# Two chunks instead of one left for the block-by-block end of a section's opening

## The chip, the cores and the metric

The kernel runs on one core of a Trainium2 chip, in one launch. The metric is the device time of a run in microseconds; the median of the timed runs is given. Lower is better.

## What is computed

The reference passes an activation `x` of 512 tokens by 1024 channels, in float32, through a chain of residual layers. Cut to what matters here:

```
layer 0:  x += 0.5 * norm(swiglu(norm(x)))      ffn0     w_gate, w_up: 1024 x 2816, w_down: 2816 x 1024
          x += norm(attention(norm(x)))         attn     w_in: 1024 x 3072 (stick-breaking and dilated heads)
          x += 0.5 * norm(swiglu(norm(x)))      ffn1
layer 1:  ffn2, mLSTM mixer (w_in: 1024 x 4112, a causal convolution of 4 taps, chunked memory), ffn3
layer 2:  x += mixer(norm(x))                   even     pooling and a diagonal state-space scan
layer 3:  x += mixer(norm(x))                   odd      gate, depthwise convolution of 31 taps, layer norm
end:      norm(x)
```

Almost all of the arithmetic is matrix products of `x` (or a hidden activation) with a weight of 1024 rows or more.

## The kernel before

**Products.** Activations are kept transposed: `x` is eight chunks of 128 channels (partitions) by 512 tokens. A weight is cut into blocks, each giving 128 output channels from all 1024 input channels: eight 128 x 128 tiles, 512 KB. To be exact enough, both factors are split into a high part (rounded to fp32r) and a low part (the rest), and each tile's product is three matmuls, high*high, low weight*high activation, high weight*low activation (`product3`, L1929 to L1931). So a block is 8 x 3 = 24 matmuls into one PSUM bank; its last one raises `blocks_done`.

**The weights' pipeline.** Blocks pass through a ring of four slots. SP (the SyncE queue) loads block b into slot b mod 4 once block b-4 is done (`load`, L1945); ACT makes the high part `wh` (`high_part`, L378); POOL makes the low part `wl` (`low_part`, L386), which raises `w_split`; the tensor engine waits for that before it takes the block. Each engine takes its work strictly in the order in which it is written, so the SILU or the copy that ACT has ahead of a `high_part` also holds that one up.

**The activations' split.** At the start of a section the eight chunks of the normalized input are made one after another: ACT makes the high part `xh` (L2199 and L2200 in the FFNs and attention, where the norm's rate is applied to the products later; L408 in the others) and POOL the low part `xl` (`split_low`, L417), which raises `xn_ready`. Between chunk 4 and chunk 5 POOL makes the low part of the section's block 3.

**A section's opening.** As the chunks arrive one by one, the first three blocks of a section (slots 0, 1 and 2) are not taken block after block but chunk by chunk, in the function `first_three`: for chunk k the six matmuls with the high activation (`three_high`, L1996 and L1997: three blocks, two matmuls each), one step behind it the three with the low activation (`three_low`, L2002). The last chunk is taken block by block (`three_last`, through `product3`): three matmuls and block 0 is done, three more and block 1, three more and block 2. `first_three` opens ten sections: the gate and up projections of ffn0 to ffn3, attn.qk, mlstm.qk, even.in, even.out, odd.in, odd.out. The output section of the memory layer (`memory_out`) and that of attention (`attention_out`) have openings of their own, which call the same helpers.

**Behind the opening** comes, in the FFNs and in attention, `spread_rate` (L1882), which brings the norm's rate into a PSUM bank; DVE copies it (L2388) and needs the copy to scale the first product. Then come block 3 and, when its slot 0 has been loaded and split again, block 4, and so on in order. In an FFN, ACT's order after the opening is: SILU of the first hidden tile (L2214), `high_part` of block 4, the hidden tile's high part (L2218), `high_part` of block 5. In mlstm.qk DVE does a convolution of four taps on each block and ACT a SILU of it before the next `high_part`. In even.out and odd.out ACT squares the new `x` chunk of block 0 before it takes block 4.

Of the kernel before, what the change touches and what calls it, by code (L numbers as in the profile page):

```python
# [15 lines left out]
KD = D // P  # L16
# [100 lines left out]
def build(nc, x_in, weights, vecs, consts, rel_bias, buckets, w_gates, pool_w, bst, cst, scratch, turn, park, out):  # L117
    ctx = ExitStack()
    with ctx:
# [1806 lines left out]
        def product3(pe, dst, q, t, in_hi, in_lo, first, last):  # L1926

            cols = slice(t * P, (t + 1) * P)
            pe.matmul(dst, wh[:, q, cols], in_hi, start=first, stop=False)  # L1929
            pe.matmul(dst, wl[:, q, cols], in_hi, start=False, stop=False)  # L1930
            return pe.matmul(dst, wh[:, q, cols], in_lo, start=False, stop=last)  # L1931
# [58 lines left out]
        def _(pe):  # L1990
            def three_high(name, k, first):
                tile = slice(k * P, (k + 1) * P)
                for s in range(3):
                    if first:
                        pe.wait_ge(w_split, BLK[name] + s + 1)
                    pe.matmul(lin[s], wh[:, s, tile], xh[:, k, :], start=first, stop=False)  # L1996
                    pe.matmul(lin[s], wl[:, s, tile], xh[:, k, :], start=False, stop=False)  # L1997

            def three_low(k):
                tile = slice(k * P, (k + 1) * P)  # L2000
                for s in range(3):
                    pe.matmul(lin[s], wh[:, s, tile], xl[:, k, :], start=False, stop=False)  # L2002

            def three_last(ks):
                for s in range(3):
                    for k in ks:
                        last = product3(pe, lin[s], s, k, xh[:, k, :], xl[:, k, :], False, k == ks[-1])
                    last.then_inc(blocks_done, 1)

            def first_three(name, key):  # L2010

                pe.wait_ge(tiles_freed, FREE0 + TILE[name])
                for k in range(KD):
                    if key in DEFERRED:
                        pe.wait_ge(x_high, X_HIGH[key] + k + 1)
                    else:
                        pe.wait_ge(hi_ready, SPLIT[key] + k + 1)
                    if k < KD - 1:
                        three_high(name, k, k == 0)
                    if k:  # L2020
                        pe.wait_ge(xn_ready, SPLIT[key] + k)
                        three_low(k - 1)
                pe.wait_ge(xn_ready, SPLIT[key] + KD)
                three_last((KD - 1,))

            def attention_out(chunks):
                for chunk in chunks:
# [14 lines left out]
            def linear(name, key=None, amid=None, begun=False):  # L2042

                if key:
                    first_three(name, key)
                    if amid:
                        amid(pe)
                if key or begun:
                    pe.wait_ge(w_split, BLK[name] + 4)
                    block_mm(pe, lin[3], 3, xh, xl)  # L2050
                with pe.Fori(1 if key or begun else 0, NBLK[name] // 4) as i:
                    for s in range(4):
                        pe.wait_ge(w_split, BLK[name] + s + 1 + 4 * i)
                        pe.wait_ge(tiles_freed, FREE0 + TILE[name] + 4 * i + s - 3)
                        block_mm(pe, lin[s], s, xh, xl)
# [23 lines left out]
            def ffn(name, idx):  # L2079
                gu, dn_ = name + ".gu", name + ".dn"  # L2080
                if idx == 0:
                    strip_tensor(pe)
                first_three(gu, name)
                if idx == 0:
                    pe.wait_ge(consts_loaded, 16)
                    square_tensor(pe, "ffn0.pre")
                spread_rate(pe, EVENT[name + ".pre"], rate_pre, 6)
                pe.wait_ge(w_split, BLK[gu] + 4)
                block_mm(pe, lin[3], 3, xh, xl)
                with pe.Fori(1, KF // 2) as i:  # L2090
                    for s in range(4):
                        pe.wait_ge(w_split, BLK[gu] + s + 1 + 4 * i)
                        if s % 2 == 0:
                            pe.wait_ge(tiles_freed, FREE0 + TILE[gu] + 4 * i + s - 2)
                        block_mm(pe, lin[s], s, xh, xl)
                pe.wait_ge(h_lo, 2 + KF * idx + DN[0] + DN[1])
                with pe.Fori(0, 2) as i:
                    for m in range(4):
                        pe.wait_ge(tiles_freed, FREE0 + TILE[dn_] + 4 * i + m - 3)
                        k0 = 0  # L2100
                        for j, n in enumerate(DN):
                            pe.wait_ge(w_split, BLK[dn_] + 3 * m + j + 1 + 12 * i)
                            if j == 2 and m == 0:
                                pe.wait_ge(h_lo, 2 + KF * (idx + 1))
                            block_mm(pe, lin[m], (3 * m + j) % 4, hh, hl, n=n, k0=k0, total=KF)
                            k0 += n
                branch_tensor(pe, name)
# [30 lines left out]
            ffn("ffn3", 3)  # L2138
            spread_rate(pe, EVENT["even.pre"], rate_pre, 6)
            even_in_tensor(pe, first_three)  # L2140
            even_tensor(pe)
            linear("even.out", "even.y")
# [526 lines left out]
```

## Time and profile before

| | |
|---|---|
| timed runs, median | 2530.04 us (2529.4, 2530.04, 2532.44) |
| profiled execution | 2523.57 us |
| its span, first to last instruction | 2521.8 us |
| tensor engine busy | 2458.4 us (97%) |
| POOL busy | 1293.0 us (51%) |
| DVE busy | 996.7 us (40%) |
| ACT busy | 976.0 us (39%) |
| mean granted clock of the tensor engine | 0.995 |

All times in the rows count from the start of the span of the one profiled execution. PE is the tensor engine's matmuls; an instruction's row gives its start, its length, engine, line, operation, what it writes and reads, and in brackets how long the engine stood idle before it and what it waited for. A matmul of 512 columns is shown with 0.39 us although the next one starts sooner, since they are pipelined. xh, xl are the parts of the activations, wh, wl those of the weights, hf the buffer of the normalized chunks.

### The profile page before, as it was taken

How to read it: one execution, taken by the hardware profiler on the slowest of the kernel's cores; microseconds unless marked ns; L12 is line 12 of the kernel's file. 1: busy time of each engine (PE TensorE's matmuls, PEld its weight loads, DVE VectorE, ACT ScalarE, POOL GpSimd, SP SyncE). 2: the span in 40 equal slices, each digit the busy share in tenths (PEclk: the TensorE clock that was granted, in tenths of full speed). 3: DMA queues.
4: the chain of work that ended last, by engine and by line, in shares of the span. 5: the costliest groups of instructions: out<-in, count | busy, mean ns of one | idle time of the engine just before them, and what ended most of it. 6: DMA issues, size and time to landing. Idle time of an engine off the chain costs nothing.

```text
span 2521.8 us, 31067 instructions
## 1 busy us (share of the span) xinstructions
PE 2458.4 (97%) x11430; PEld 1996.1 (79%) x11430; DVE 996.7 (40%) x1504; ACT 976.0 (39%) x1308; POOL 1293.0 (51%) x705
## 2 busy tenths in 40 slices
PE   8999999989999999999999999999999999999997
PEld 6888888866888888888888778778888887877676
DVE  3222413146522211322231551445222693834885
ACT  5333333366533333433333333435333433233543
POOL 5555545320565554555554544226555555256974
PEclk9999999999999999999999999999999999999999
DMA  4333433210233333233333223113333455333741
GB/s 142 100 93 99 148 103 117 92 34 1 92 96 95 100 100 108 84 95 96 100 101 107 77 84 97 36 34 101 100 91 100 140 160 178 112 100 89 193 130 67
DMA packets 79995, 251.67 MB, mean 100 GB/s; under 512 B 9732, under 2 KB 14212, under 8 KB 79789
## 3 DMA queue, kind: packets, MB, share of 16 engines
q1 hardware_dynamic: 72384, 235.55, 30.2%
q10 hardware_dynamic: 6684, 11.90, 1.5%
q0 software_dynamic: 848, 3.15, 0.4%
q8 instruction: 52, 0.85, 0.1%
q14 instruction: 27, 0.21, 0.0%
HBM read 237.54 MB, written 15.25 MB: 100 GB/s over the span
## 4 chain that ended last, share of the span: by engine, by line
PE 85%; DVE 4%; POOL 3%; ACT 3%; issue 2%; DMA 2%; SPq 0%; DVEq 0%; ACTq 0%; POOLq 0%
PE banks L1929 23%; PE banks L1931 23%; PE banks L1930 23%; POOL wl_sb L386 2%; DMA raw_sb<-weights 1%; PE banks L1996 1%; PE banks L1997 1%; POOL xl_sb L417 1%; PE banks L2068 1%; PE banks L2070 1%; PE banks L2069 1%; PE banks L2002 1%; PE banks L1875 1%; PE banks L1882 1%; PE banks L963 1%
## 5 line engine op out<-in xcount | busy, mean ns | idle before, releaser
L386 POOL TENSOR_TENSOR wl_sb<-raw_sb,wh_sb 128x1024 fp32r<-128x1024 f32 x401 | 967.3, 2414 | 847.6 <-ACT wh_sb L378 846.0
L1929 PE MATMUL banks<-xh_sb,wh_sb 128*128 128x512 f32 x2055 | 803.8, 391 | 5.9 <-POOL wl_sb L386 5.4
L1930 PE MATMUL banks<-xh_sb,wl_sb 128*128 128x512 f32 x2055 | 800.0, 389 | 0.0
L1931 PE MATMUL banks<-xl_sb,wh_sb 128*128 128x512 f32 x2055 | 799.8, 389 | 0.0
L378 ACT ACTIVATE wh_sb<-raw_sb 128x1024 fp32r<-128x1024 f32 x401 | 425.0, 1060 | 771.2 <-DMA raw_sb<-weights 761.2
L1929 PEld LDWEIGHTS banks<-xh_sb,wh_sb 128*128 128x128 f32 x2055 | 385.7, 188 | 98.5 <-issue 10.4
L1931 PEld LDWEIGHTS banks<-xl_sb,wh_sb 128*128 128x128 f32 x2055 | 385.8, 188 | 80.3
L1930 PEld LDWEIGHTS banks<-xh_sb,wl_sb 128*128 128x128 f32 x2055 | 385.8, 188 | 79.6 <-issue 0.2
L1931 PE MATMUL banks<-hl_sb,wh_sb 128*128 128x512 f32 x704 | 273.9, 389 | 0.0
L1930 PE MATMUL banks<-hh_sb,wl_sb 128*128 128x512 f32 x704 | 273.9, 389 | 0.0
L1929 PE MATMUL banks<-hh_sb,wh_sb 128*128 128x512 f32 x704 | 273.9, 389 | 0.0
L2397 DVE TENSOR_TENSOR hf_sb<-banks,rstd_sb 128x512 f32<-128x512 f32 x88 | 60.8, 691 | 382.2 <-PE banks L1931 376.9
L2439 POOL TENSOR_TENSOR hl_sb<-hf_sb,hh_sb 128x512 f32 (+1 forms) x88 | 113.8, 1294 | 130.5 <-ACT hh_sb L2218 130.5
L2394 DVE TENSOR_TENSOR hf_sb<-banks,rstd_sb 128x512 f32<-128x512 f32 x88 | 60.9, 691 | 261.1 <-PE banks L1931 259.8
L2218 ACT ACTIVATE hh_sb<-hf_sb 128x512 f32 (+1 forms) x88 | 55.6, 632 | 257.2 <-DVE hf_sb L2400 257.2
L1929 PEld LDWEIGHTS banks<-hh_sb,wh_sb 128*128 128x128 f32 x704 | 132.1, 188 | 27.6
L1931 PEld LDWEIGHTS banks<-hl_sb,wh_sb 128*128 128x128 f32 x704 | 132.2, 188 | 27.4
L1930 PEld LDWEIGHTS banks<-hh_sb,wl_sb 128*128 128x128 f32 x704 | 132.1, 188 | 27.3
L417 POOL TENSOR_TENSOR xl_sb<-hf_sb,xh_sb 128x512 fp32r<-128x512 f32 x80 | 108.7, 1381 | 77.3 <-ACT xh_sb L408 30.2
L2400 DVE TENSOR_TENSOR hf_sb<-hf_sb 128x512 f32<-128x512 f32 x88 | 130.4, 1482 | 6.4 <-ACT hf_sb L2214 3.6
L2304 DVE SCALAR_TENSOR_TENSOR xs_sb<-banks,vecs_sb,x_sb 128x512 f32<-128x512 f32 x32 | 24.0, 750 | 251.4 <-ACT hf_sb L2176 251.3
L1996 PE MATMUL banks<-xh_sb,wh_sb 128*128 128x512 f32 x249 | 103.4, 415 | 14.8 <-issue 7.8
(387 smaller groups left out, 2582.8 us busy)
## 6 DMA issues: line engine op xcount, KB each, us to landing
raw_sb<-weights SPq DMA_DIRECT2D x404, 512.0 KB, 3.5
park<-xs_sb ACTq DMA_DIRECT2D x12, 512.0 KB, 4.2
mix_sb<-scratch SPq DMA_DIRECT2D x16, 258.0 KB, 5.5
hf_sb<-scratch SPq DMA_DIRECT2D x16, 258.0 KB, 5.3
mix_sb<-park SPq DMA_DIRECT2D x4, 1024.0 KB, 6.6
scratch<-scratch ACTq DMA_DIRECT2D x1, 2560.0 KB, 11.9
scratch<-mix_sb SPq DMA_DIRECT2D x8, 259.5 KB, 2.8
x_sb<-x_in SPq DMA_DIRECT2D x8, 256.0 KB, 8.8
```

What stands on the lines that cost most here:

```text
L378: act.activation(wh[:, slot, :], raw[:, slot, :], ACT.Copy).then_inc(w_hi, 1)
L386: pool.tensor_tensor(wl[:, slot, :], raw[:, slot, :], wh_f[:, slot, :], ALU.subtract).then_inc(w_split, 1)
L417: pool.tensor_tensor(xl[:, c, :], hf[:, c, :], xh_f[:, c, :], ALU.subtract).then_inc(xn_ready, 1)
L1929: pe.matmul(dst, wh[:, q, cols], in_hi, start=first, stop=False)
L1930: pe.matmul(dst, wl[:, q, cols], in_hi, start=False, stop=False)
L1931: return pe.matmul(dst, wh[:, q, cols], in_lo, start=False, stop=last)
L1996: pe.matmul(lin[s], wh[:, s, tile], xh[:, k, :], start=first, stop=False)
L2218: act.activation(at(hh, 2 * i + s), ht[:, s, :], ACT.Copy).then_inc(h_hi, 1)
L2394: dve.tensor_tensor(sg[:, s, :], lin[2 * s], rstd[:, :], ALU.mult).then_inc(gate_scaled, 1)
L2397: dve.tensor_tensor(ht[:, s, :], lin[2 * s + 1], rstd[:, :], ALU.mult).then_inc(tiles_freed, 2)
L2400: dve.tensor_tensor(ht[:, s, :], ht[:, s, :], sg[:, s, :], ALU.mult).then_inc(h_mul, 1)
L2439: pool.tensor_tensor(at(hl, 2 * i + s), ht[:, s, :], at(hh_f, 2 * i + s), ALU.subtract).then_inc(h_lo, 1)
```

## The change

In `first_three` the two last chunks (6 and 7) are taken block by block at the end, in place of chunk 7 alone. Block 0 now ends with six matmuls in a row (three of chunk 6, three of chunk 7), then block 1, then block 2. The loop over the chunks no longer issues chunk 6's high and low matmuls, and its last pass issues nothing but its waits. Number and kind of matmuls stay as they are, and each bank is still opened by chunk 0 and closed by chunk 7.

```
-                    if k < KD - 1:
+                    if k < KD - 2:
                         three_high(name, k, k == 0)
-                    if k:
+                    if 0 < k < KD - 1:
                         pe.wait_ge(xn_ready, SPLIT[key] + k)
                         three_low(k - 1)
                 pe.wait_ge(xn_ready, SPLIT[key] + KD)
-                three_last((KD - 1,))
+                three_last((KD - 2, KD - 1))
```

`three_last` itself is unchanged: `for s in range(3)`, `for k in ks`, a `product3`, and after the last k `blocks_done` is raised.

## Rows read from the trace of the kernel before

**Rows 1.** The page, busy time and share of the span

```profile
PE 2458.4 (97%) x11430; PEld 1996.1 (79%) x11430; DVE 996.7 (40%) x1504; ACT 976.0 (39%) x1308; POOL 1293.0 (51%) x705
```

**Rows 2.** Waits of PE by line: total us, times, longest

```profile
PE banks L1929 <- POOL wl_sb L386: 5.4, 9, 1.1
```

**Rows 3.** Timeline of PE, attn.qk's opening: start, length, instruction

```profile
396.01 0.39 PE L1996 MATMUL banks<-xh_sb,wh_sb 128*128 128x512 f32 x1
...
397.37 1.53 PE L2002 MATMUL banks<-xl_sb,wh_sb 128*128 128x512 f32 x6
399.05 0.50 PE L1929 MATMUL banks<-xh_sb,wh_sb 128*128 128x512 f32 x1
```

**Rows 4.** Timeline of POOL, attn.qk's opening

```profile
395.22 3.77 POOL L417 TENSOR_TENSOR xl_sb<-hf_sb,xh_sb 128x512 fp32r<-128x512 f32 x3
```

**Rows 5.** Timelines of POOL and PE, ffn0's opening

```profile
23.75 5.21 POOL L417 TENSOR_TENSOR xl_sb<-hf_sb,xh_sb 128x512 fp32r<-128x512 f32 x3
...
28.78 1.52 PE L2002 MATMUL banks<-xl_sb,wh_sb 128*128 128x512 f32 x6
```

**Rows 6.** Timelines of POOL and PE, openings of mlstm.qk, even.in, even.out, odd.in

```profile
1420.76 3.78 POOL L417 TENSOR_TENSOR xl_sb<-hf_sb,xh_sb 128x512 fp32r<-128x512 f32 x3
...
1425.11 1.52 PE L2002 MATMUL banks<-xl_sb,wh_sb 128*128 128x512 f32 x6
...
2107.63 3.78 POOL L417 TENSOR_TENSOR xl_sb<-hf_sb,xh_sb 128x512 fp32r<-128x512 f32 x3
...
2111.84 1.52 PE L2002 MATMUL banks<-xl_sb,wh_sb 128*128 128x512 f32 x6
...
2247.98 5.47 POOL L417 TENSOR_TENSOR xl_sb<-hf_sb,xh_sb 128x512 fp32r<-128x512 f32 x4
...
2309.34 3.82 POOL L417 TENSOR_TENSOR xl_sb<-hf_sb,xh_sb 128x512 fp32r<-128x512 f32 x3
...
2313.79 1.52 PE L2002 MATMUL banks<-xl_sb,wh_sb 128*128 128x512 f32 x6
```

**Rows 7.** Timeline of PE, block 4: ffn1, mlstm.qk, even.in, even.out, odd.in, odd.out

```profile
693.87 0.49 PE L1929 MATMUL banks<-xh_sb,wh_sb 128*128 128x512 f32 x1 [0.49 <-POOL wl_sb L386]
...
1435.25 0.49 PE L1929 MATMUL banks<-xh_sb,wh_sb 128*128 128x512 f32 x1 [1.14 <-POOL wl_sb L386]
...
2121.41 0.50 PE L1929 MATMUL banks<-xh_sb,wh_sb 128*128 128x512 f32 x1 [0.57 <-POOL wl_sb L386]
...
2271.02 0.51 PE L1929 MATMUL banks<-xh_sb,wh_sb 128*128 128x512 f32 x1 [0.67 <-POOL wl_sb L386]
...
2323.19 0.49 PE L1929 MATMUL banks<-xh_sb,wh_sb 128*128 128x512 f32 x1 [0.40 <-POOL wl_sb L386]
...
2486.55 0.50 PE L1929 MATMUL banks<-xh_sb,wh_sb 128*128 128x512 f32 x1 [0.54 <-POOL wl_sb L386]
```

**Rows 8.** Timeline of ACT, the split of block 4 in even.out

```profile
2267.44 1.06 ACT L378 ACTIVATE wh_sb<-raw_sb 128x1024 fp32r<-128x1024 f32 x1 [2.50 <-DMA raw_sb<-weights]
```

**Rows 9.** Timelines of DVE and ACT, ffn1 behind its opening

```profile
687.95 0.69 DVE L2388 COPY rstd_sb<-banks 128x512 f32<-128x512 f32 x1 [8.85 <-PE banks L1882]
...
689.68 0.64 ACT L2214 ACTIVATE hf_sb<-hf_sb 128x512 f32<-128x512 f32 x1 [6.41 <-DVE hf_sb L2394]
690.22 1.04 ACT L378 ACTIVATE wh_sb<-raw_sb 128x1024 fp32r<-128x1024 f32 x1
```

**Rows 10.** Timeline of PE, the state kernels of the even layer

```profile
2182.20 0.34 PE L1407 MATMUL banks<-mix_sb 128*32 128x32 f32 x4 [2.01 <-DVE hf_sb L1608]
```

**Rows 11.** Stretches: length, PE busy (count), granted clock, DMA share, GB/s

```profile
2246.40:2248.30 1.90, 0.00 (x1) 1.00 0.41 86
2248.30:2251.70 3.40, 3.40 (x15) 1.00 0.27 106
1405.60:1410.50 4.90, 1.17 (x10) 1.00 0.00 0
1410.90:1414.30 3.40, 3.40 (x10) 0.51 0.00 0
```

## The prediction

> **What bounds the kernel now.** I began with the busy table of the page. The tensor engine is busy for 97% of the span [rows 1], so a matmul that is delayed costs its delay, unless the engine would have waited for something soon after; and time can be won only at the engine's own waits. The waits grouped by line come next [rows 2]: the single largest kind behind the product line L1929 is the low part of a weight block made on POOL, 9 times, 5.4 us in all. I then located these nine in time. Eight of them stand in sections that open with `first_three`, each time at block 4, the first block that needs a slot which `first_three` has freed [rows 7]; the ninth is in the memory layer's output section, which doesn't use it. Last I read the ten openings themselves (ten calls: four FFNs, attn.qk, mlstm.qk, even.in, even.out, odd.in, odd.out), asking for each whether the tensor engine or POOL's split of the activations is the later one when the last chunk comes.
>
> The reader is to see two kinds. In attn.qk the six last low matmuls begin at 397.37 and the last product only at 399.05, which is the moment when POOL's third split of a run of three ends, 395.22 + 3.77 = 398.99 [rows 3, 4]. So here POOL is the later one: all that the tensor engine had in hand (high and low of chunk 6) has been done while POOL made chunk 7. ffn1, ffn2 and ffn3 repeat this to within 0.1 us. In the other sections POOL is done before the tensor engine gets there: in mlstm.qk it ends at 1424.54, the last product starts at 1425.11 + 1.36 = 1426.47 [rows 6].
>
> **The unit.** Six matmuls take 397.37 - 396.01 = 1.36 us, 0.227 us each, though one is shown with 0.39 us because neighbours overlap by 0.16 us [rows 3]. The change neither adds nor removes a matmul. It takes nine (six high, three low, of chunk 6) out of the stretch ahead of the wait for all eight low chunks and puts them behind it: 9 x 0.227 = 2.04 us. Nothing else of the change costs an instruction; the wait for low chunk 7 of the loop merges into the one for 8.
>
> **What is lost, where POOL is late.** In attn.qk the wait still ends at 398.99; behind it 18 matmuls stand where 9 stood. The cover of chunk 7's split is gone, and the section ends 2.04 us later. Behind the waiting matmul are all of the engine's work, the spread of the rate (L1882) and through it DVE's copy of it. In the same way ffn1, ffn2, ffn3: 4 x 2.04 = 8.16 us. In ffn0 POOL ends at 23.75 + 5.21 = 28.96; 0.06 us on, as in attn.qk, the first product could start at 29.02. It started at 28.78 + 1.36 = 30.14 [rows 5]. A restart after a wait costs some 0.10 us (0.49 to 0.50 shown for the first matmul, 0.39 for the others [rows 3, 7]). End: 29.02 + 0.10 + 2.04 - 30.14 = +1.02 us. Sum of losses 9.2 us.
>
> **What is lost, where POOL is early.** With chunk 6's high part gone, low chunk 5 begins where that high part began, 1.36 us ahead of the rows with six low matmuls, and takes 0.68 us. mlstm.qk: done at 1425.11 - 1.36 + 0.68 = 1424.43, POOL at 1424.54, so a start at 1424.60 and an end shifted by 1424.60 + 0.05 + 2.04 - 1426.47 = +0.22 (half a restart, since the engine hardly runs dry). even.in: POOL 2107.63 + 3.78 = 2111.41, the end +0.41 by the same sum with a whole restart. odd.in: POOL 2309.34 + 3.82 = 2313.16, engine 2313.11, the end +0.16 [rows 6]. even.out: POOL has ended its splits at 2247.98 + 5.47 = 2253.45, long before; nothing. odd.out repeats even.out; nothing.
>
> **What is won.** Block 0 used to be complete with 6 matmuls to go, now with 12; block 1 with 6 in place of 3. Against the end of the opening, block 0 is ready 1.36 us earlier and block 1 0.68 us earlier, so slot 0 is reloaded, split on ACT and POOL earlier. That is what the waits at block 4 hang on. In even.out the ACT split of block 4 is released by the load itself [rows 8], the load by block 0. To the shown idle time 0.16 us of overlap and 0.10 of restart are added, as a matmul that doesn't wait starts before its predecessor's shown end. Each wait is at most 1.14 + 0.16 = 1.30 us, and what arrives 1.36 less the shift earlier covers it: in mlstm.qk the low part comes 1.36 - 0.22 = 1.14 us sooner and is wanted 0.22 later, so 1.36 against 1.30, just enough. Net gains [rows 7]: mlstm.qk 1.14 + 0.26 - 0.22 = 1.18; even.in 0.57 + 0.26 - 0.41 = 0.42; even.out 0.67 + 0.26 = 0.93; odd.in 0.40 + 0.26 - 0.16 = 0.50; odd.out 0.54 + 0.26 = 0.80. Together 3.8 us. even.in's could be lost or doubled: a 2.01 us wait for DVE's state chain stands behind it [rows 10], and its start hangs on the SP queue, where the table loads sit between the loads of blocks 4 and 5; bounds 0 and 1.0, value 0.42 as this is what the tensor engine itself brings.
>
> **The FFNs win nothing.** ffn1 to ffn3 have such a wait too, 0.49 us in ffn1 [rows 7]. But there ACT's queue holds the first SILU ahead of the split of block 4: DVE's copy of the rate (687.95, from the spread behind the opening), its product, SILU at 689.68 after 6.41 us of waiting, and directly behind it, with no wait of its own, the split at 690.22 [rows 9]. All of that moves with the end of the opening by 2.04 us, so the wait at block 4 stays.
>
> **Sum.** 8.16 + 1.02 - 3.83 = +5.35 us. The profiled execution took 2523.57 us around a span of 2521.8; the median of the timed runs is 2530.04, 6.5 us over it, and I put that difference in both kernels. 2530.04 + 5.35 = 2535.4 us.
>
> **A clock that could fall.** In mlstm.qk's opening the granted clock fell to 0.51 (1.2 GHz) for 3.4 us after a stretch of 4.9 us in which the engine was busy 1.17; it did 10 matmuls there, where 15 fit at the full 2.4 GHz. Yet after 1.90 us of idling ahead of even.out it stayed at 1.00 [rows 11]. The change makes a new pattern: in attn.qk and ffn1 to ffn3 the engine comes to low chunk 5 at 396.01 while POOL ends that chunk near 396.49, works 0.68 us and waits to 399.05. About 0.4 and 1.5 us dry, nearly 2 of 3 us. A fall would cost (15 - 10) x 0.227 = 1.1 us, or up to 1.7 us if every matmul of 3.4 us takes double. By the idle rows alone that is a coin with few falls, so the sum takes none. [...]
>
> **The rivals.**
> (a) The clock falls behind some of the four new waits: 1.1 to 1.7 us each, 2536.5 for one, up to 2542 for four. For it: the fall in mlstm.qk; against: the 1.90 us at even.out. 0.19.
> (b) Not slower: the FFNs' waits at block 4 go as well. The place is ACT's split at 690.22; if the load's landing and not SILU decided, the low part would come 2.04 - 0.68 = 1.36 us sooner against the demand, more than 0.49 + 0.16, and each of three gives back 0.49 + 0.26 = 0.75, 2.3 us in all: +3.1 us, 2533.1, within 0.2%. It decides if the split can start at the landing rather than behind SILU; the row without a wait speaks against it. With a second source of the same size (even.in at its 1.0) 2532.5. 0.14.
> (c) The earlier release brings nothing, as another thing is late at block 4 (DVE's convolution ahead of ACT's split in mlstm.qk, POOL's own queue): +9.2 us, 2539.2. Against it: ACT waits 2.50 us for the load in even.out [rows 8]. 0.08.
> (d) The change gains outright: the delays of 9.2 us are taken up by later waits that don't move with them, and the 3.8 us stay: 2526.2. For it nothing but that 0.8 to 2.5 us waits exist in attention and even; they hang on work that the tensor engine itself starts. 0.03.
>
> **How the numbers follow.** The forecast has 0.56, with its own range 2533.5 to 2537.5. A measurement can tell 0.2%, 5.06 us, which puts the line at 2535.1, next to the forecast: of its 0.56 I put 0.31 above the line, 0.25 below. Slower is 0.31 + 0.18 of (a) + 0.08 of (c) = 0.57; within 0.2% is 0.25 + 0.14 of (b) + 0.01 of (a), where smaller terms outweigh its fall, = 0.40; faster is (d), 0.03. The range 2531.5 to 2540.5 holds (b), (c) and up to three falls of (a).
>
> **What would show it.** In attn.qk and ffn1 to ffn3: a wait of the tensor engine of about 1.5 us that ends with POOL L417, then 18 matmuls of L1929 to L1931; in ffn1 to ffn3 the wait at block 4 unchanged. In the other five sections the wait at block 4 gone. Granted clock 1.00 behind the new waits. The forecast is wrong if the openings' ends move by other than 2.04 us, if a wait at block 4 stays in mlstm.qk or even.out, or if a clock falls.

## The result, and the profile after

| | before | changed |
|---|---|---|
| timed runs, median | 2530.08 us (15 runs, 2526.18 to 2533.92) | 2538.62 us (15 runs, 2535.16 to 2542.57) |
| profiled execution | 2523.57 us | 2538.01 us |
| its span | 2521.8 us | 2536.3 us |
| its mean granted clock | 0.995 | 0.992 |

The ratio changed to before is 1.0031, 95% interval [1.0023, 1.0039]: slower by 7.8 us (5.8 to 9.9), clear of the 0.2% line. I had forecast 2535.4 us, slower by 5.35.

The two profiles differ by 14.5 us, much more than the timed runs. Both must be read with their clock: a second profile of the kernel before (e5 below) has a span of 2526.1 us at 0.994.

First the waits of the tensor engine by line, of the changed kernel: who waited for whom, total us, times, longest. [Rows 2] had one line with 5.4 us, 9 times.

```profile
PE banks L1929 <- POOL xl_sb L417: 6.1, 4, 1.5
...
PE banks L1734 <- DMA mix_sb<-scratch: 3.2, 2, 2.6
...
PE banks L1929 <- POOL wl_sb L386: 2.5, 5, 0.7
...
PE banks L2002 <- POOL xl_sb L417: 1.9, 4, 0.5
...
PE banks L1396 <- DMA mix_sb<-turn: 1.1, 1, 1.1
```

Two new lines have come: four waits of 1.5 us for the last low chunk and four of 0.5 us for low chunk 5. The waits for low weights have gone from nine to five: the three FFNs and the memory layer's output have theirs still, and one of 0.36 us in ffn0's down projection is new.

The timeline of the tensor engine in attn.qk's opening answers to [rows 3], that of POOL to [rows 4]; the opening starts 1.93 us later here, so times are to be compared after subtracting that:

```profile
397.27 0.84 PE L2002 MATMUL banks<-xl_sb,wh_sb 128*128 128x512 f32 x3
398.59 0.93 PE L2002 MATMUL banks<-xl_sb,wh_sb 128*128 128x512 f32 x3 [0.47 <-POOL xl_sb L417]
401.05 0.47 PE L1929 MATMUL banks<-xh_sb,wh_sb 128*128 128x512 f32 x1 [1.52 <-POOL xl_sb L417]
```

```profile
397.13 3.76 POOL L417 TENSOR_TENSOR xl_sb<-hf_sb,xh_sb 128x512 fp32r<-128x512 f32 x3
```

POOL's run of three ends at 400.89 and the first product starts at 401.05, 15.06 us behind the opening's first matmul, where it was 399.05 - 384.06 = 14.99 before. So the wait ends when it did, and 18 matmuls follow in place of 9.

The timelines of the tensor engine and of ACT in ffn1 answer to the first of [rows 7] and to [rows 9]:

```profile
700.31 0.49 PE L1929 MATMUL banks<-xh_sb,wh_sb 128*128 128x512 f32 x1 [0.49 <-POOL wl_sb L386]
```

```profile
696.11 0.63 ACT L2214 ACTIVATE hf_sb<-hf_sb 128x512 f32<-128x512 f32 x1 [8.49 <-DVE hf_sb L2394]
696.65 1.04 ACT L378 ACTIVATE wh_sb<-raw_sb 128x1024 fp32r<-128x1024 f32 x1
```

SILU waited 2.08 us longer (8.49 against 6.41), the split stands right behind it again, and the wait at block 4 is 0.49 us as before.

The lengths of stages, from the first matmul of an opening to that of the next, with busy time and granted clock, of the changed kernel: attn, ffn1, ffn2, mlstm, ffn3, even.in in this order (length, busy and count, granted clock, DMA share, GB/s).

```profile
385.99:674.03 288.04, 275.65 (x1348) 0.99 0.21 64
674.03:1043.94 369.91, 367.42 (x1652) 1.00 0.32 97
1043.94:1420.47 376.53, 370.31 (x1660) 1.00 0.31 95
1420.47:1680.69 260.22, 257.99 (x1217) 0.99 0.21 65
1733.39:2110.07 376.68, 370.36 (x1659) 1.00 0.37 116
2110.07:2261.61 151.54, 146.08 (x809) 0.98 0.42 129
```

and the same stages of the kernel before:

```profile
384.06:669.69 285.63, 275.13 (x1347) 0.99 0.20 64
669.69:1037.53 367.84, 367.23 (x1651) 1.00 0.31 97
1037.53:1410.49 372.96, 368.63 (x1660) 1.00 0.31 96
1410.49:1671.66 261.17, 257.90 (x1216) 0.99 0.20 65
1724.33:2097.39 373.06, 368.63 (x1660) 1.00 0.37 118
2097.39:2248.30 150.91, 145.90 (x809) 0.98 0.42 129
```

ffn1 is the clean case: +2.07 us, forecast 2.04. ffn2 (+3.57) and ffn3 (+3.62) have 1.5 us on top. The memory layer won 0.95 us, forecast 1.18. What is on top in ffn2 and ffn3 is the clock. The stretches are the double wait and the 3.4 us behind it in ffn2, the same two in ffn1, and the 3.4 us behind it in ffn3; they answer to [rows 11].

```profile
1056.00:1058.90 2.90, 0.99 (x4) 0.99 0.00 0
1058.90:1062.30 3.40, 3.31 (x8) 0.51 0.00 0
686.10:689.00 2.90, 0.99 (x4) 1.00 0.00 0
689.10:692.50 3.40, 3.40 (x15) 1.00 0.20 36
1748.40:1751.80 3.40, 3.35 (x8) 0.51 0.02 5
```

The two double waits are equal: busy 0.99 of 2.90 us. Behind that in ffn2 the clock was 0.51 (1.2 GHz) for 3.4 us and 8 matmuls were done, behind that in ffn1 it was 1.00 and 15 were done. ffn3 is as ffn2. That is rival (a): the clock fell in two of the four openings.

What the early openings won is seen best at the first matmul of block 5, which stands behind the wait at block 4. In even.out, whose openings start at 2248.30 (before) and 2261.61 (changed) and where the clock was at 1.00 in both, it is this:

```profile
2276.63 0.39 PE L1929 MATMUL banks<-xh_sb,wh_sb 128*128 128x512 f32 x1
```

```profile
2288.98 0.39 PE L1929 MATMUL banks<-xh_sb,wh_sb 128*128 128x512 f32 x1
```

Block 5 starts 28.33 us into the opening before and 27.37 us in the changed kernel, 0.96 us sooner; forecast 0.93.

### The profile page after: what moved, and what is told of

It is laid out like the page before. It is cut to its first block, busy times and chain, and to the rows that moved or that the text cites. A ratio compares the mean times of both kernels' runs of the same rounds, so it can differ in the third digit from the quotient of the medians.

```text
span 2536.3 us, 31077 instructions
## 1 busy us (share of the span) xinstructions
PE 2466.3 (97%) x11430; PEld 2001.2 (79%) x11430; DVE 999.4 (39%) x1504; ACT 976.0 (38%) x1308; POOL 1294.5 (51%) x705
## 4 chain that ended last, share of the span: by engine, by line
PE 86%; DVE 4%; POOL 3%; ACT 2%; issue 2%; DMA 2%; SPq 0%; DVEq 0%; POOLq 0%; ACTq 0%
PE banks L1929 24%; PE banks L1930 23%; PE banks L1931 23%; PE banks L1996 1%; PE banks L1997 1%; POOL wl_sb L386 1%; PE banks L2002 1%; PE banks L2068 1%; PE banks L2070 1%; PE banks L2069 1%; DMA raw_sb<-weights 1%; PE banks L1875 1%; POOL xl_sb L417 1%; PE banks L1882 1%; PE banks L963 1%
## 5 line engine op out<-in xcount | busy, mean ns | idle before, releaser
L1929 PE MATMUL banks<-xh_sb,wh_sb 128*128 128x512 f32 x2085 | 816.6, 392 | 8.4 <-POOL xl_sb L417 6.1
L1930 PE MATMUL banks<-xh_sb,wl_sb 128*128 128x512 f32 x2085 | 812.6, 390 | 0.0
L1931 PE MATMUL banks<-xl_sb,wh_sb 128*128 128x512 f32 x2085 | 812.4, 390 | 0.0
L1929 PEld LDWEIGHTS banks<-xh_sb,wh_sb 128*128 128x128 f32 x2085 | 392.2, 188 | 101.7 <-issue 19.7
L1931 PEld LDWEIGHTS banks<-xl_sb,wh_sb 128*128 128x128 f32 x2085 | 392.1, 188 | 81.6
L1930 PEld LDWEIGHTS banks<-xh_sb,wl_sb 128*128 128x128 f32 x2085 | 392.4, 188 | 80.8 <-issue 0.2
L2400 DVE TENSOR_TENSOR hf_sb<-hf_sb 128x512 f32<-128x512 f32 x88 | 138.4, 1573 | 6.0 <-ACT hf_sb L2214 3.2
L2214 ACT ACTIVATE hf_sb<-hf_sb 128x512 f32<-128x512 f32 x88 | 55.7, 633 | 148.2 <-DVE hf_sb L2394 148.2
```

Of the source, the lines that this page charges most:

```text
L2214: act.activation(sg[:, s, :], sg[:, s, :], ACT.Silu).then_inc(gate_act, 1)
L2400: dve.tensor_tensor(ht[:, s, :], ht[:, s, :], sg[:, s, :], ALU.mult).then_inc(h_mul, 1)
```

## The experiments

Ratios are to the runs of the kernel before on the same chip (2528.48 us, 26 runs, for e1 to e4; 2529.14 us, 17 runs, for e5 to e8).

### e1, e2: one half of the change each

```
-                    if k < KD - 2:
+                    tail = 2 if key not in DEFERRED else 1        # e2: if key in DEFERRED
+                    if k < KD - tail:
...
-                three_last((KD - 2, KD - 1))
+                three_last(range(KD - tail, KD))
```

> The two-chunk end only in the five sections where POOL is done before the tensor engine (mlstm.qk, even.in, even.out, odd.in, odd.out); ffn0 to ffn3 and attn.qk as before. My theory: the gain alone, the waits at block 4 gone in these five: -3.8 us against before by the sum; since the changed kernel's trace gives back even.in's and odd.in's part to transfers that land later, -1.5 to -3.8. Rival 'the earlier release brings nothing': 0. Rival 'clock': falls there are neither more nor fewer than before, the mean granted clock as before's.

> The two-chunk end only in the five sections where the tensor engine catches up with POOL (ffn0 to ffn3, attn.qk). My theory: +9.2 us from the matmuls that now stand behind POOL's last split, plus 1.1 to 1.7 us for each fall of the clock behind the new waits, two in a run: +11 to +13, mean granted clock lower than before's. If no clock falls: +9.2. Rival 'the loss is small': +5 or less.

e1: 2526.13 us (11 runs), ratio 0.9991 [0.9982, 0.9999], -2.3 us. e2: 2540.75 us (5 runs), ratio 1.0048 [1.0035, 1.0061], +12.1 us. The halves add up to +9.8 us, the changed kernel's two measurements are +7.8 and +8.9 (e6), which agrees within the intervals. So the change was two changes with opposite signs: where POOL is early it pays, where POOL is late it costs, and the two kinds can be told apart in the profile of before. In e2's profile the waits for the two kinds of low parts stand side by side:

```profile
PE banks L1929 <- POOL xl_sb L417: 6.9, 5, 1.5
PE banks L1929 <- POOL wl_sb L386: 5.2, 9, 1.1
```

All nine waits for low weights are there again, as in [rows 2], and those for low activations have come; its ffn1 is 369.90 us long, as the changed kernel's 369.91. In e1's profile the waits for low weights are 2.6 us, 5 times. e1's gain came out at the lower part of what I expected, and its mean clock is 0.9924 (11 runs) against 0.9935 (26 runs), so it isn't "as before's"; why is open (below). It is also no higher than e2's 0.9926 (5 runs), though only e2 has the new waits: the mean clock of a run doesn't single them out, the stretches in the profiles do.

### e3: who holds up block 4 in the FFNs

This is e1 with ACT's split of block 4 taken ahead of the first SILU:

```
+                if idx:
+                    high_part(act, gu, 1)
                 silu(0, 0)
-                if idx:
-                    high_part(act, gu, 1)
                 hidden_high(0, 0)
```

> As e1, and in ffn1 to ffn3 ACT splits block 4 before the first SILU. My theory: SILU in ACT's queue held that split, so the three waits at block 4 (0.49 us each) go and it is 3 x 0.75 = 2.3 us faster than e1, -4 to -6 us against before. Rival: the load's landing decides, then the waits stay or shrink by less than half and it equals e1, or is slower because SILU, and the hidden tiles behind it, start 0.8 us later.

2525.83 us (12 runs), ratio 0.9986 [0.9977, 0.9994], -3.5 us against before, 1.3 less than e1, where intervals overlap. The stage shows it better than the run. ACT's split of block 4 in ffn1 is now released by the load, and the first SILU comes behind it:

```profile
687.88 1.06 ACT L378 ACTIVATE wh_sb<-raw_sb 128x1024 fp32r<-128x1024 f32 x1 [7.15 <-DMA raw_sb<-weights]
688.96 1.28 ACT L2215 ACT_TABLE_LOAD   x1
690.25 0.63 ACT L2215 ACTIVATE hf_sb<-hf_sb 128x512 f32<-128x512 f32 x1
```

The waits at block 4 are gone in all three, one is left in the whole kernel (the memory layer's output):

```profile
PE banks L1929 <- POOL wl_sb L386: 0.6, 1, 0.6
```

and ffn1 takes 367.05 us, 0.79 less than before; I had 0.75. In ffn2 and ffn3 block 4 starts 23.55 us into the opening, where it was 24.18 and 24.19 before, so the gain is there too. The whole stages (373.15 and 373.19 us) don't show it: in this profile the clock was at 0.50 over their last 3.6 us, in before's over none and 0.4 us of them. The split had been held by ACT's order, not by the load, and rival (b) is refuted.

### e4: a filled wait

This is the changed kernel with six matmuls put into the wait of attn.qk and ffn1 to ffn3, into a bank that nobody reads:

```
+                if key in DEFERRED[1:]:
+                    for n in range(6):
+                        pe.matmul(banks[:, 5, :], wh[:, 0, 0:P], xh[:, n, :], start=True, stop=True)
                 pe.wait_ge(xn_ready, SPLIT[key] + KD)
```

> The changed kernel, with six more matmuls in attn.qk and ffn1 to ffn3 ahead of the wait for the last low chunk, into a bank that nobody reads: they fill 1.36 us of the 1.5 us wait and delay nothing. If the falls of the clock come from the new waits, these falls are gone behind the four openings, the mean clock is as before's and the time is 1 to 4 us under the changed kernel's (+5 against before). If the falls have another cause, the time is the changed kernel's, +8.

2535.03 us (8 runs), ratio 1.0027 [1.0017, 1.0037], +6.8 us. The timeline of the tensor engine in ffn2's opening (L2025 is the filler), then the stretches of wait and what follows in ffn2 and in ffn3, then the lengths of ffn1, ffn2 and ffn3:

```profile
1053.80 0.94 PE L2002 MATMUL banks<-xl_sb,wh_sb 128*128 128x512 f32 x3 [0.47 <-POOL xl_sb L417]
1054.57 1.55 PE L2025 MATMUL banks<-xh_sb,wh_sb 128*128 128x512 f32 x6
1056.21 0.50 PE L1929 MATMUL banks<-xh_sb,wh_sb 128*128 128x512 f32 x1
```

```profile
1056.20:1059.60 3.40, 3.39 (x15) 1.00 0.20 30
...
1744.50:1747.90 3.40, 3.33 (x15) 1.00 0.10 14
```

```profile
671.35:1041.21 369.86, 368.79 (x1658) 1.00 0.31 97
1041.21:1416.23 375.02, 370.25 (x1666) 1.00 0.31 95
1729.56:2104.64 375.08, 370.19 (x1665) 1.00 0.37 117
```

The first product starts where it did (15.00 us into the opening in ffn2, 15.05 in the changed kernel), the clock stays at 1.00 in all four openings, and ffn2 and ffn3 are 1.51 and 1.60 us shorter than the changed kernel's: 2.06 and 2.02 us over before, the matmuls alone. One profile with four openings without a fall stands against three profiles of unfilled waits (changed, e2, e6) with 2, 2 and 3 falls in four openings. In these openings that shows the mechanism and its price, 1.5 us a fall. The whole run doesn't settle it: it is 1.0 and 2.0 us under the changed kernel's two measurements, with overlapping intervals, and the mean clock is 0.9918 over 8 runs, not 0.9935 as I expected (the changed kernel has 0.9916 over 15 runs).

### e5, e6: both kernels once more

No edit.

> The kernel before, unchanged, for a second profile. My theory: the 14.5 us between the two first profiles are more than the 8.5 us of the timed runs because the clock's falls lie elsewhere in every execution (0.995 in that profile of before, 0.9935 on the mean of 26 runs). Then this profile's span is some us over 2521.8 wherever the clock is lower, and the lengths of stages without a fall repeat to 0.1 us. If the difference were the kernel's, span and clock would repeat.

> The changed kernel, unchanged, on the chip on which e7 and e8 run. +7 to +9 us against before, as before; its profile tells whether a clock's fall in an opening is there again (theory: in 1 to 3 of the 4) and whether odd.in's first wait for the moved taps and even.in's wait for the turned u are longer than before's again (theory: yes, what the earlier release wins there is given back to transfers).

e5: span 2526.1 us at 0.994. Stages with equal clock repeat (ffn1 367.85 against 367.84 us, ffn3 373.09 against 373.06), those with other falls don't (even.out 53.54 against 52.45 us, even.in 153.16 against 150.91). e6: 2540.21 us (7 runs), ratio 1.0035 [1.0024, 1.0046], +8.9 us. In its profile the clock fell behind the new wait in attn.qk, ffn2 and ffn3, three of four:

```profile
401.10:404.50 3.40, 3.40 (x9) 0.50 0.11 14
1059.90:1063.30 3.40, 3.20 (x8) 0.50 0.00 0
1749.40:1752.80 3.40, 3.40 (x9) 0.50 0.02 5
```

and in e2's in attn.qk and ffn2, two of four:

```profile
400.50:403.90 3.40, 3.40 (x9) 0.50 0.02 5
1059.30:1062.70 3.40, 3.15 (x8) 0.50 0.00 0
```

e6's even.in is 150.27 us long; the changed kernel's was 151.54, before's 150.91 and 153.16, e2's (where even.in is as before) 150.70. So the 0.63 us that even.in seemed to lose in the first comparison can't be put down to the change: differences of that size come and go from profile to profile. The same holds for the moved taps of odd.in (3.2 us of waits in the changed kernel, 3.0 in e6, but 3.5 in e2, whose odd.in is as before; 2.2 in before). I had expected these two to be the change's; e2 has them without it.

### e7, e8: the low part of block 3 behind chunk 7

```
-                if c == 4 and section:
+                if c == (KD - 1 if key in DEFERRED else 4) and section:
                     low_part(pool, section, 0)
```

in `split_low`, for the changed kernel (e7) and for e3 (e8). It holds in ffn0 to ffn3 and attn.qk (`DEFERRED`).

> The changed kernel, with POOL's split of block 3 moved from behind chunk 4 to behind chunk 7 in ffn0 to ffn3 and attn.qk, so that the last low chunk is made 1.3 to 2.4 us sooner. My theory: the loss was the two-chunk end standing behind POOL's last split; with that earlier, the end of each of the four openings comes about 1.3 us sooner than in the changed kernel and ffn0's 1 us sooner, and the new wait is too short for the clock to fall: 6 to 9 us under the changed kernel, -1 to +1 us against before. Rival: the loss is the order of the matmuls itself, whatever POOL does: then as e6.

> e3 (two-chunk end in the five sections where POOL is early, block 4 split ahead of the first SILU in ffn1 to ffn3) and POOL's split of block 3 behind chunk 7 in ffn0 to ffn3 and attn.qk. My theory: a further 0.4 us in each of four openings, -1.7 us against e3, so -4 to -7 us against before. Rival: ACT's high part of chunk 7 is as late as POOL was, then it equals e3.

e7: 2530.12 us (11 runs), ratio 1.0002 [0.9992, 1.0011]: as a whole the change costs nothing any more, though all its matmuls stand where they stood. POOL and the tensor engine in ffn1's opening (that starts at 670.67):

```profile
676.89 2.62 POOL L417 TENSOR_TENSOR xl_sb<-hf_sb,xh_sb 128x512 fp32r<-128x512 f32 x2 [1.34 <-ACT hf_sb L2200]
680.57 3.77 POOL L417 TENSOR_TENSOR xl_sb<-hf_sb,xh_sb 128x512 fp32r<-128x512 f32 x3 [1.07 <-ACT hf_sb L2200]
684.30 2.39 POOL L386 TENSOR_TENSOR wl_sb<-raw_sb,wh_sb 128x1024 fp32r<-128x1024 f32 x1
```

```profile
684.48 0.47 PE L1929 MATMUL banks<-xh_sb,wh_sb 128*128 128x512 f32 x1 [1.02 <-POOL xl_sb L417]
```

POOL is done 13.67 us into the opening in place of some 14.9; it now waits for ACT, so of the 2.4 us that were moved 1.25 arrive. The wait of the tensor engine is one of 1.02 us, and ffn1 takes 368.67 us, 0.83 over before against 2.07. What POOL is sooner by, the loss is smaller by: it hangs on how late POOL's last chunk comes. The clock was at 1.00 behind all four waits. The 0.83 us that stay in ffn1 are balanced in the whole run by the gains of the early sections. So the order still costs something where POOL's split of block 3 stands behind chunk 7: block 3 starts 18.83 us into ffn1's opening here and 17.52 in e8, which has the same order on POOL and the old end.

e8: 2522.03 us (5 runs), ratio 0.9964 [0.9950, 0.9978], -9.1 us against before (5.6 to 12.6): it beats both kernels, by more than the -4 to -7 I had given it. ffn1, ffn3 and the memory layer in its profile:

```profile
668.74:1035.34 366.60, 366.60 (x1652) 1.00 0.31 97
1720.75:2092.84 372.09, 368.28 (x1660) 1.00 0.38 118
1407.93:1668.16 260.23, 258.05 (x1216) 0.99 0.21 65
```

In ffn1 the tensor engine is busy for all of 366.60 us, 1.24 less than before (e3: 0.79, so 0.45 for the move; forecast 0.4). The low end of the interval lies in the range expected; what is over it was not traced. The move was not run alone on the kernel before, so what it gives there is known only from such stages.

## Why the prediction came out as it did

- **The unit and the four late openings**: right. 2.04 us each were forecast; 2.07 us in ffn1 (changed), 2.06 in ffn1 of e2, 2.02 in the filled ffn1, 2.06 and 2.02 in the filled ffn2 and ffn3, where the clock doesn't interfere. In attn.qk, where the changed kernel's clock didn't fall either, block 3 starts 20.07 us into the opening in place of 17.97. ffn0's 1.02 us can't be checked closely: with the new end (changed, e2, e4, e6) block 3 starts 25.26 to 26.04 us into its opening, with the old one (before, e1, e3, e5) 24.73 to 25.87.
- **The FFNs win nothing at block 4**: right, 0.49 us before and after; e3 showed why, by taking SILU out of the way.
- **The gains**: right in size. By the start of block 5 in the opening, in profiles of equal clock there: mlstm 0.96 (changed against before; forecast 1.18: block 3 starts 0.34 us later, where 0.22 was forecast), even.in 0.34 (changed against before) and 0.51 (e6 against e2; forecast 0.42), even.out 0.96 (0.93), odd.in 0.37 (changed against before) and 0.57 (against e5; forecast 0.50), odd.out 0.75 (e7 against before) and 1.06 (e7 against e2; forecast 0.80). Behind the openings transfers and the clock vary by more than that, above all in odd.in. As a whole e1 gives 2.3 us [0.3, 4.6] for 3.83, so the whole of the gain is not shown to reach the end.
- **"By the idle rows alone that is a coin with few falls, so the sum takes none"**: this is the step that failed; by the prediction's own sign ("or if a clock falls") the forecast was wrong, and 2538.62 us lies outside its own range of 2533.5 to 2537.5 and inside the wider one. In the three profiles with unfilled double waits (changed, e2, e6) the clock fell behind 7 of 12, at 1.5 us (I had 1.1 to 1.7; the 1.1 is too low, since of the 10 matmuls of [rows 11] two began ahead of the stretch). Four openings with 7/12 of a fall give 3.5 us on the mean, an estimate from three profiles: 5.35 + 3.5 = 8.9 us, against 7.8 and 8.9 measured. The whole runs leave room in that sum: with the falls filled (e4) the kernel is still +6.8 us [4.3, 9.4] for 5.35. I had given rival (a) 0.19 where it should have been the forecast. The mistake, as I see it, was to weigh the 1.90 us of idling ahead of even.out, one stretch without a fall, as strongly as the fall itself; the new waits come in pairs, with 0.9 us of work between them, like those ahead of mlstm.qk, behind which it had fallen. The Trainium skill, "TensorE: Matmul & The Clock Gate", section "HAM oscillation — how this bites in real kernels", tells of a kernel whose waits of some 3 to 5 us between bursts each brought the engine back to half rate. The gaps here, 0.5 and 1.5 us, are far shorter, and a fall followed in seven openings of twelve; in ffn1 none of the three profiles has one. So what the page says of long waits is no safe line for short ones.
- **Rivals (b), (c), (d)**: (b) refuted by e3, (c) by e1 and by the waits at block 4 that went, (d) by e2, whose losses come through to the end.
- **Open**: mean clocks lie lower in nearly every variant (0.9915 in e3, 0.9918 in e4, 0.9924 in e1) than in before (0.9933 over 43 runs), though e1 and e3 add no wait. In their profiles the clock is at 0.50 for 6.8 us around the start of mlstm.qk and for 10.1 us around that of odd.in, where both profiles of before have 3.4 us in the first place and none or 3.4 in the second. Why was not settled, nor whether it holds in most runs; a profile shows one execution, and falls in odd.in and even.out move from one to the next (even.out 52.45 and 53.54 us in two profiles of one kernel). Nor was it tried why ffn2's wait met a fall in all three profiles and ffn1's equal one in none.

## What to carry over

Before work is put behind a wait, look which engine is later at that wait. Work moved from ahead of it costs its full length where the waiting engine was the early one, and little or nothing where it was the late one (in mlstm.qk block 3 started 0.34 us later); the same edit can be right for one caller of a function and wrong for the next, and each caller has its own rows. If the wait is there anyway, look what the late engine does in front of it that nobody needs yet: moving that took 1.24 us off ffn1 in the changed kernel (e7) and 0.45 us in e8, and the whole of the changed kernel's loss.

## What the runs showed of the hardware

A wait need not be long to cost clock. Two dry stretches of 0.5 and 1.5 us with 0.9 us of matmuls between them were followed by 3.4 us at a granted clock of 0.50 to 0.51 (1.2 GHz) in 7 of 12 cases (changed kernel, e6, e2), and a single one of 1.0 us (e7) by none in its profile's four openings. Filling 1.4 of the 1.5 us with matmuls whose result nobody reads saved 1.5 us a stage where the clock would have fallen (ffn2 375.02 against 376.53 us). Two profiles of the same kernel differed by 4.3 us in span (2521.8 and 2526.1), 2.25 us of it in even.in, where the clock was at half for some 3 us longer, and 1.09 us in even.out, which had one fall in the second and none in the first.
